# One core, GLA, retention and expert layer: picks behind the splits, gathers in another order, upper parts first

## What is computed

```python
h = layer_norm(alpha * x + hybrid_mixer(x))     # projection w_in, GLA and retention heads, w_out
q = (h @ w_q).reshape(t, 8, 2, 128)             # the peer layer: product keys
scores = einsum('thpd,hpkd->thpk', q, subkeys)
# top 16 of each half, top 16 of the sums: 128 experts of 16384 for each token, gates by softmax
act = gelu(einsum('tkd,td->tk', u_tab[experts], h))
out = layer_norm(alpha * h + einsum('tk,tkd->td', gates * act, v_tab[experts]))
```

## Time and profile before

| | us |
|---|---|
| median of 3 runs | 1937.12 |
| lowest, highest | 1935.56, 1940.14 |
| the profiled execution, time | 1930.02 |
| the profiled execution, span | 1928.2 |

### The profile page before, as it was taken

One profiled execution on the slowest core, in us unless ns is written; L12 is line 12 of the kernel. 1 busy time (PEld: TensorE's weight loads), 2 busy tenths in 40 slices (PEclk: granted clock), 3 DMA queues, 4 the chain that ended last, 5 costly groups with the idle time before them and its releaser, 6 DMA issues.

```text
span 1928.2 us, 34656 instructions
## 1 busy us (share of the span) xinstructions
PE 1902.5 (99%) x10830; PEld 1664.7 (86%) x10830; DVE 1340.2 (70%) x2305; ACT 989.5 (51%) x1518; POOL 1436.9 (75%) x962
## 2 busy tenths in 40 slices
PE   9999999999999999999999999999999999999996
PEld 8999888888998888888888888888788888888885
DVE  1844012214688877765889998997788888888887
ACT  5544434435445556657455555555555555555553
POOL 6877878887878899989788878786476576666631
PEclk9999999999999999999999999999999999999998
DMA  9555657577869888787977777777899999999983
GB/s 302 174 153 164 205 149 226 176 232 181 212 148 206 185 190 192 166 189 182 251 172 176 173 172 174 167 177 208 305 328 339 333 329 343 357 352 367 359 311 114
DMA packets 197497, 440.60 MB, mean 229 GB/s; under 512 B 29408, under 2 KB 40544, under 8 KB 196272
## 3 DMA queue, kind: packets, MB, share of 16 engines
q1 hardware_dynamic: 181712, 384.40, 69.6%
q0 software_dynamic: 14416, 50.61, 7.6%
q10 hardware_dynamic: 1296, 4.65, 0.7%
HBM read 426.79 MB, written 12.78 MB: 228 GB/s over the span
## 4 chain that ended last, share of the span: by engine, by line
PE 78%; POOL 10%; issue 7%; DMA 3%; DVE 1%; ACT 1%; POOLq 0%; SPq 0%; DVEq 0%; ACTq 0%
PE ps L1817 27%; PE ps L1772 17%; PE ps L1773 9%; PE ps L1512 7%; PE ps L1514 7%; PE ps L1513 7%; POOL u_lo L1429 6%; POOL w_lo L1391 4%; PE ps L1754 3%; DMA v_raw<-in_peer_v 2%; DMA u_raw<-in_peer_u 1%; PE ps L1628 1%; PE ps L1737 0%; DVE u_t L1055 0%; PE ps L1508 0%
## 5 line engine op out<-in xcount | busy, mean ns | idle before, releaser
L1429 POOL TENSOR_TENSOR u_lo<-u_t,u_hi 128x512 fp32r<-128x512 f32 x512 | 653.8, 1300 | 127.5 <-ACT u_hi L637 125.2
L1772 PE MATMUL ps<-xT,u_hi 128*128 128x512 f32 x2048 | 724.3, 397 | 0.6 <-POOL u_lo L1429 0.4
L1773 PE MATMUL ps<-xT,u_lo 128*128 128x256 f32 x2048 | 572.9, 280 | 0.0
L1391 POOL TENSOR_TENSOR w_lo<-raw,w_hi 128x1024 fp32r<-128x1024 f32 x174 | 431.2, 2493 | 99.6 <-ACT w_hi L506 93.2
L637 ACT ACTIVATE u_hi<-u_t 128x512 fp32r<-128x512 f32 x512 | 321.2, 632 | 349.8 <-DVE u_t L1055 348.6
L1772 PEld LDWEIGHTS ps<-xT,u_hi 128*128 128x128 f32 x2048 | 384.2, 188 | 88.2 <-issue 0.9
L1055 DVE STREAM_TRANSPOSE u_t<-u_raw 128x512 f32<-128x512 f32 x512 | 355.5, 702 | 97.5 <-PE ps L1773 60.5
L1773 PEld LDWEIGHTS ps<-xT,u_lo 128*128 128x128 f32 x2048 | 386.7, 189 | 0.0
L506 ACT ACTIVATE w_hi<-raw 128x1024 fp32r<-128x1024 f32 x175 | 184.9, 1059 | 273.7 <-PE ps L1514 261.1
L1454 POOL DMA_INDIRECT sp_rows<-in_peer_v,sp_at x128 | 180.1, 1407 | 152.8 <-DVE far_sum L1268 133.3
L1817 PE MATMUL ps<-v_lo,m_hi 128*128 128x512 f32 x882 | 270.2, 375 | 0.0
(11 more groups left out here) (233 smaller groups left out, 2688.3 us busy)
## 6 DMA issues: line engine op xcount, KB each, us to landing
u_raw<-in_peer_u SPq DMA_DIRECT2D x512, 256.0 KB, 4.8
v_raw<-in_peer_v SPq DMA_DIRECT2D x252, 512.0 KB, 6.2
raw<-in_w_in SPq DMA_DIRECT2D x111, 512.0 KB, 3.8
raw<-in_w_out SPq DMA_DIRECT2D x32, 512.0 KB, 4.8
raw<-in_w_peer_q SPq DMA_DIRECT2D x128, 128.0 KB, 4.3
act_dram<-act_w ACTq DMA_DIRECT2D x4, 1024.0 KB, 6.6
act_dram<-far_act SPq DMA_DIRECT2D x62, 64.0 KB, 5.0
x_again<-in_x SPq DMA_DIRECT2D x1, 2048.0 KB, 8.1
```

Of the source, the lines that this page charges most:

```text
L1391: pool.tensor_tensor(w_lo[:, k, :], raw[:, k, :], w_hi[:, k % HI_RING, :].bitcast(F32), ALU.subtract).then_inc(lo_done, 1)
L1429: pool.tensor_tensor(u_lo[:, r, :], u_t[:, r, :], u_hi[:, r, :].bitcast(F32), ALU.subtract).then_inc(ulo_done, 1)
L1772: pe.matmul(acc, u_hi[:, r, c], xT[:, :, kt, :], start=kt == 0, stop=False)
L1773: ins = pe.matmul(acc[:, 0:T], u_lo[:, r, c], xT_hi[:, kt, :], start=False, stop=kt == KT - 1)
```

## The change

It has six places.

- **v_low:** the picks stand behind both halves' low parts.
- **Gathers:** GpSimd gathers two rows (S_AHEAD) before the gates and the nine activations, the other three of the first five behind them.
- **GpSimd at the end:** a multiplication and an addition of one column each, between the last gather and the second norm.
- **h1_rows:** the four operations on 2048 columns become eight on 1024, and the n-th waits until step n of group O_END+1 is done; h1_made is raised by the sixth and the eighth.
- **First norm:** for the first two slices TensorE transposes into two banks, ScalarE writes the high parts straight from there with gain and shift, and writes the scaled values for the low part afterwards; TensorE runs the upper products (w_hi and w_lo with the high part of the input) of both slices, transposes on, and then runs the lower ones (w_hi with the low part).
- **Head:** the same split of step 0 of group 0, with the second transposition in between.

```diff
+S_AHEAD = 2
...
+        def first_bank(k):
+            return bank(2 if k else 4)[:, 0:T]
...
+        def act_first_turn(act):
+            for k in range(2):
+                act.wait_ge(first_tr, k + 1)
+                act.activation(xT_hi[:, k, :], first_bank(k), ACT.Identity, bias=ln_rows[:, 1, k:k + 1], scale=ln_rows[:, 0, k:k + 1]).then_inc(first_hi, 1)
+            for k in range(2):
+                ins = act.activation(bank(4)[:, k * T:(k + 1) * T], first_bank(k), ACT.Identity, bias=ln_rows[:, 1, k:k + 1], scale=ln_rows[:, 0, k:k + 1])
+            ins.then_inc(tr_hi, 1)
...
             act.wait_ge(ln1_in, 128)
-            for c in range(4):
+            act_first_turn(act)
+            for c in range(1, 4):
                 act_scaled_turn(act, c)
...
             for a in range(TT):
-                dve.tensor_tensor(part(h1_rows[:, a, :], 0, KT), in_perm(n_perm[:, a, :], 0, KT), part(ln1g_sb[:], 0, KT), ALU.mult)
+                for f in (0, KT // 2):
+                    dve.wait_ge(step_free, used(O_END + 1, 2 * a + f // 8))
+                    dve.tensor_tensor(part(h1_rows[:, a, :], f, KT // 2), in_perm(n_perm[:, a, :], f, KT // 2), part(ln1g_sb[:], f, KT // 2), ALU.mult)
             dve.drain()
             for a in range(TT):
-                dve.tensor_tensor(h1_rows[:, a, :], h1_rows[:, a, :], ln1b_sb[:], ALU.add).then_inc(h1_made, 1)
+                for h in range(2):
+                    c = slice(h * D // 2, (h + 1) * D // 2)
+                    dve.wait_ge(step_free, used(O_END + 1, 4 + 2 * a + h))
+                    ins = dve.tensor_tensor(h1_rows[:, a, c], h1_rows[:, a, c], ln1b_sb[:, c], ALU.add)
+                ins.then_inc(h1_made, 1)
...
                 dve.tensor_tensor(v_lo[:, 2 * s, :], v_raw[:, 2 * s, :], v_hi[:, 2 * (s % 2), :].bitcast(F32), ALU.subtract)
-                for n, j in added:
-                    row_add(n, j)
                 dve.wait_ge(m_hi_done, ii * 4 + s + 1)
...
+                for n, j in added:
+                    row_add(n, j)
...
-            for k in range(S_SLOTS):
+            for k in range(S_AHEAD):
                 row_gather(k)
...
             for k in range(S_PAIR):
                 act_gather(k)
+            for k in range(S_AHEAD, S_SLOTS):
+                row_gather(k)
...
+            pool.drain()
+            pool.tensor_tensor(pool_spare, sp_gate[:, 0:1], sp_gate[:, 1:2], ALU.mult)
+            pool.drain()
+            pool.tensor_tensor(pool_spare, sp_gate[:, 0:1], sp_gate[:, 1:2], ALU.add)
             ln_power(3, slice(0, 1))
...
+            def upper_four(g, kt):
+                for w in (w_hi, w_lo):
+                    for n in range(4):
+                        c = slice(kt * COL + n * P, kt * COL + (n + 1) * P)
+                        o = ps[:, 2 * (g % 2) + n // 2, (n % 2) * T:(n % 2 + 1) * T]
+                        pe.matmul(o, w[:, 0, c], xT_hi[:, kt, :], start=kt == 0 and w is w_hi and n % 2 == 0, stop=False, skip_group_check=True)
...
             turn(x_sb, 0, 0, *ready(0))
-            for k in range(STEPS):
+            acc_wait(0)
+            pe.wait_ge(lo_half, 1)
+            pe.wait_ge(tr_hi, 1)
+            upper_four(0, 0)
+            turn(x_sb, 0, 1, *ready(1))
+            pe.wait_ge(tr_lo, 1)
+            lower_four(0, 0)
+            pe.wait_ge(lo_done, 1)
+            upper_four(0, 1)
+            lower_four(0, 1).then_inc(step_free, 1)
+            for k in range(1, STEPS):
...
-            turned_group(O_END, steps_n, n_perm, 2, lambda c: (n_block, 2 * c + 2 if c < 2 else 2 * (c // 2) + 4), lead=4)
+            blocks = lambda c: (n_block, 2 * c + 2 if c < 2 else 2 * (c // 2) + 4)
+            pe.wait_ge(*blocks(0))
+            for k in range(2):
+                for a in range(TT):
+                    ins = pe.transpose(first_bank(k)[:, a * P:(a + 1) * P], by_tile(n_perm, a, k), ident)
+                ins.then_inc(first_tr, 1)
+            pe.sem_inc(tr_done, 1)
+            turn(n_perm, 2, 1, *blocks(1))
+            pe.wait_ge(lo_done, STEPS * O_END + 1)
+            for kt in range(2):
+                pe.wait_ge(first_hi, kt + 1)
+                upper_four(O_END, kt)
+            for c in (2, 3):
+                turn(n_perm, 2, c, *blocks(c))
+            pe.wait_ge(tr_lo, 17)
+            for kt in range(2):
+                ins = lower_four(O_END, kt)
+            ins.then_inc(step_free, 1)
+            turn(n_perm, 2, 4, *blocks(4))
+            for k in range(1, STEPS):
+                pe.wait_ge(tr_lo, 16 + k + 1)
+                steps_n(O_END, (k,))
+                if k + 4 < 8:
+                    turn(n_perm, 2, k + 4, *blocks(k + 4))
```

More of the change, by code:

```diff
@@ L228, in build @@
         gmax = small[:, 184:200]
+        pool_spare = small[:, 199:200]
         LOW_ROW = 32
@@ L263, in build @@
         tr_done, tr_hi, tr_lo = sem("tr_done"), sem("tr_hi"), sem("tr_lo")
+        first_tr, first_hi = sem("first_tr"), sem("first_hi")
         glrw_hi, glrw_lo, glr_done, glrT_done, logit_done = (sem(n) for n in ("glrw_hi", "glrw_lo", "glr_done", "glrT_done", "logit_done"))
@@ L1542, in steps_n, with lower_four @@
                     ins.then_inc(step_free, 1)
+            def upper_four(g, kt):
[4 more added lines that the diff above has]
+                        pe.matmul(o, w[:, 0, c], xT_hi[:, kt, :], start=kt == 0 and w is w_hi and n % 2 == 0, stop=False, skip_group_check=True)
+            def lower_four(g, kt):
+                for n in range(4):
+                    c = slice(kt * COL + n * P, kt * COL + (n + 1) * P)
+                    o = ps[:, 2 * (g % 2) + n // 2, (n % 2) * T:(n % 2 + 1) * T]
+                    ins = pe.matmul(o, w_hi[:, 0, c], xT_lo[:, kt, :], start=False, stop=False, skip_group_check=True)
+                return ins
             def steps_t(g, ks=range(STEPS)):
```

## The result

| | before | changed |
|---|---|---|
| median of 16 runs each, us | 1936.43 | 1941.14 |
| lowest, highest | 1932.04, 1940.14 | 1937.44, 1944.31 |
| the profiled execution, time (span) | 1930.02 (1928.2) | 1942.01 (1939.9) |

The ratio is 1.0024, with a 95% interval of 1.0015 to 1.0032: slower by 4.7 us (2.9 to 6.2). The forecast was +9.2 and 1946.3; the direction was right, the size was twice what was measured.

What follows compares the result with a forecast made beforehand. TensorE was taken as the bound, busy 1902.5 of 1928.2 us. Terms +14.0 +2.0 -0.5 -0.5 -1.8 -4.0 = +9.2 on 1930.02 gave 1939.2; with 7.1 more, 1946.3, range 1940.5 to 1951.

Steps and rivals of the forecast that it cites:

- The stall, +14.0: Before group O_END+2: halved first-norm sums delay SyncE's copy and weight loads; TensorE resumes at 523.0 instead of 509.0, +14.0 us.
- Case B: Rival: weights land beside the copy, 6.3 after it instead of 10.3, with 0.5 less slow clock: 1941.8; chance 0.15.
- The clock, +2.0: After the hole before group O_END+2, TensorE restarts at the 1.2 GHz level: +2.0 us, bounds 0 and 3.0.
- The first norm, -0.7: At the first norm's transposition, TensorE's wait for the low part's subtract goes: -0.7 us, counted inside the 14.0.
- The head, -0.5: At the kernel's start, upper products first let a transposition move forward and step 1 start earlier: -0.5 us.
- Contention, -0.74: At the first norm's sums, halves stretch GpSimd's low parts less, so TensorE's wait goes: -0.74 us, within the 14.0.
- The tail, -4.0: At the end, GpSimd's 4.19 us pause before its first add moves behind the last gather: -4.0 us.
- Gathers -1.8 and picks -0.5: Value tiles: later row gathers remove the 1.70 wait and a small one, -1.8 us; later picks remove the 0.52, -0.5.
- The offset of 7.1: The kernel before's shown median, 1937.12, lies 7.1 above its profiled execution; the same was added to the changed kernel's 1939.2.
- D: Rival: weights of group O_END+2 arrive in time, so only gains of 8.2 stay: 1928.9; chance 0.05.
- C: Rival: the end add's pause stays (+4.0), or slow clock and load backlog take 2 to 4 more: 1950.3; chance 0.15.
- E: Rival, no difference: Case B's short landing without slow clock, all gains in full: near 1940; chance 0.07.

Runs made afterwards that it cites:

- the changed kernel with 128 KB: The changed kernel with one extra 128 KB DRAM-to-DRAM copy in each value tile: 1943.12 us, ratio 1.0031 against the kernel before without load.
- the added wait: The early halves' kernel, with GpSimd's first addition at the end waiting for VectorE's second shift: 1935.81 us, ratio 0.9942.
- the 128 KB load: One extra 128 KB DRAM-to-DRAM copy per value tile in both kernels: before 1943.79 us, changed 1943.12; ratios 1.0032 and 1.0031 against before without load.
- the later sets: The kernel before and the changed kernel timed again, both unaltered: ratio 1.0041 in the second set, 1.0044 in the fourth.
- the early halves: The changed kernel with its eight half sums behind steps 4, 5, 5, 6, 7 of group O_END and 0, 0, 1 of O_END+1: 1934.15 us, ratio 0.9942.

## Why the prediction was right or wrong

The forecast put the changed kernel 9.2 above the one before, and the medians differ by 4.7. The mechanism came out: the stall, its place in SyncE's queue and the slow clock behind it. The step that failed is the last one, "I put the same difference on it": it took the difference of two single executions for that of the medians. The two profiled times differ by 12.0, more than forecast, and the medians by 4.7, as before's profiled execution lies 6.4 below its median and the changed one's 0.9 above. Of the terms, those of the value tiles were too small and that of the tail too large. The parts in turn:

**The stall, +14.0: right.** Every mark of the chain landed within 0.4 us, the hole is 15.0, where the forecast's marks give 15.5, and the sums alone cost 16.2 (13.0 to 19.3) where the terms gave 16.7. That the marks fit so closely is in part luck: this execution was 1.07 late at the first mark already, and a larger gain in the norm made up for it. The row that carried it was the single copy of the earlier trace rows: 10.32 there, 10.05 now, and 9.9 to 10.3 in four other traces with the stall; in the fifth, the changed kernel with 128 KB, it was 12.6 and the hole 17.5. Case B's ground, pieces that land beside the copy, fell, and the run with the copy moved shows that the copy is some 6 of that time.

**The clock, +2.0: right, a little low.** From 523.16 to 529.06 a product starts each 0.213 us instead of each 0.120: 27 products took 5.9 instead of 3.2, so 2.7 us were lost.

**The first norm, -0.7: too small.** From the first mark to the transposes of turn 4 it is 11.1 instead of 12.2, 1.1 won.

**The head, -0.5: not shown.** The forecast let step 1 hang on "a transposition which moves forward by 0.7"; it moved forward into a wait for the transfer of x. The first mark is at 450.0 in the mean of the nine traces without the edit and at 449.9 in that of the eleven with it, so the +1.1 of the table is no effect of the edit.

**Contention, -0.74: as said.** In the groups of w_q TensorE waits for w_lo in the hole only. Without the sums' edit it waits 0.38 and 1.24 for w_lo beside the whole sums, and the norm's gain is eaten: its stretch is 109.6 again.

**The tail, -4.0: mis-sized, -2.4 in the trace, -2.7 alone.** In nine of the ten traces with this edit and without the added wait the rest is 2.3 to 2.4 shorter, in the tenth 3.3. The step was "the next late one is VectorE's last write, ending 1920.42": it took VectorE's time as fixed while GpSimd's operations moved onto it. The earlier trace rows had the effect in the forecast's own hand.

**Gathers -1.8 and picks -0.5: mis-sized together, -3.5 and -3.1 alone.** Together they were forecast at 2.3; the value tiles are 3.5 shorter in the two first traces, 4.2 in the means of all but the head's (557.8 and 553.6), and 13.7 under the 128 KB load. For the gathers by themselves the interval still holds -1.8. The step that failed here is the count of "the waits at 1357.63 and 1715.39" as if they were fixed: they are those of one execution. A wait of 0.52 in one place of 124 tiles is a sample of how close VectorE's order runs to the transfers, and other executions draw others: 0.85 at 1680 us and 1.52 at 1718 in one, ten of 8.2 in all under load.

**The offset of 7.1: the failed step.** "I put the same difference on it" took the distance of before's profiled execution (1930.02; the lowest of its 16 runs is 1932.04) from its median as a property of both kernels. The changed kernel's profiled execution is 0.9 above its own median. Theory P could explain a part: what makes usual runs of before slower than its trace could be what the change removes. For the result's own runs that stays open. In the later sets the difference was 7.9 and 8.5, near the 9.2, and there the two profiled executions of before lie within 0.3 of the median of their own runs.

**The sum** of the parts timed alone is 16.2 - 3.5 - 3.1 - 2.7 = +6.9 (the head left out, as its interval holds 1, and the norm not timed alone), between the result's +4.7 and the later +7.9 and +8.5, but with intervals of 2 to 3 us either way on each part it cannot tell these apart. Of the rivals, B's figure (1941.8) is nearest to the result, but its mechanism, a landing 6.3 behind the store, is refuted by 10.05; D's sum of gains (8.2) met the -8.1 in part by luck, as its terms are off both ways, and its condition was not met; C's pause didn't stay; E rests on B's landing.

## What to carry to other kernels

Before an operation is tied to a later step, read what stands behind the instruction that waits for it, in every queue: here a copy for a later stage stood in front of weights that TensorE wanted next, and a wait that cost VectorE nothing cost TensorE 15 us. Putting work that nobody waits for behind work that TensorE waits for can be worth more than the waits of one trace show, since it can take away a dependence on late data; judge such an edit by how the stage's length varies over executions. Do not carry the distance of one profiled execution from its median over to another kernel. And a gain at one of two engines that stretch each other's operations has to be charged with what its operations do beside the other's.

## What the runs showed of the hardware

VectorE's operations stretch beside GpSimd's by about a whole instruction of GpSimd: a 128x1024 sum of VectorE took 1.22 with GpSimd idle and 3.3 beside its 128x1024 operations of 2.4; a one-column operation took 1.21 instead of 0.15 beside a 128x512 one. The Trainium skill, "SBUF — State Buffer", section "Terms", says that the port pair which the two share is held for the full instruction and that the loser blocks. By that rule halving an operation can double its waits, and the early halves agree in direction: 26 us instead of 16.

GpSimd's pause ahead of its first add at the end is not of the place: it is 4.19 in all nine traces without the two one-column operations and 0.16 in ten of the eleven with them (in the other the add waits for VectorE). In those a pause of 6.4 to 7.6 stands ahead of the small multiplication, behind the last gather. Only the pair was tried, and that the two pauses have one cause is argued. The Trainium skill, "GPSIMD Engine Reference", section "2.1 Instruction dispatch", gives approximately 6 us for the first call to a freshly loaded kernel; the traces have 4.19 and 6.4 to 7.6, and no run here shows whether they are such a call.

TensorE's start is not the same in each execution of one kernel: four transposes at 4.76 took 1.06 in one trace of the changed kernel and at 4.49 took 0.63 in another, and step 1 began at 11.99 and 10.99; over all 20 traces it began at 10.79 to 13.43.
